# Block products over ten feature tiles in place of eight, with each column's weights in a chunk of its own

## The reference

```python
# first block
y = (o.astype(z.dtype) * jax.nn.silu(z)) @ w_out
x = x + rmsnorm(y, g_post[i])
# second block, for l in range(2)
y = jnp.concatenate([a_out, c_out, m_out], axis=-1) * jax.nn.silu(gate)
o = y @ w_o[l]
x = x + rmsnorm_2(o, post_norm_g[l])
```

## Time and profile before

| what | value |
|---|---|
| median of three runs | 2197.26 us (2196.68 to 2197.3) |
| the profiled execution, its own time | 2197.51 us |
| span of the profiled execution | 2195.7 us |
| TensorE busy | 2178.5 us (99%) |
| VectorE busy | 1524.7 us (69%) |
| ScalarE busy | 837.5 us (38%) |
| GpSimd busy | 211.3 us (10%) |
| mean granted TensorE clock | 0.999 of full speed |

### The profile page before, as it was taken

How to read it: one execution, slowest core, us unless ns; L and a number is a source line. 1 busy time by engine, 2 the same in 40 slices (tenths; PEclk the granted TensorE clock), 3 DMA queues, 4 the chain that set the end, 5 groups by cost and what they waited for, 6 DMA issues and landing times.

```text
span 2195.7 us, 27821 instructions
## 1 busy us (share of the span) xinstructions
PE 2178.5 (99%) x10428; PEld 1818.9 (83%) x10428; DVE 1524.7 (69%) x2224; ACT 837.5 (38%) x1307; POOL 211.3 (10%) x215
## 2 busy tenths in 40 slices
PE   8999999999999999999999999999999999999998
PEld 7888888888888888888888888888888888888887
DVE  6677788888988543567677778786434677677665
ACT  6433433453345421334333533444213443435221
POOL 0100000114420100000000053201000000000000
PEclk9999999999999999999999999999999999999999
DMA  7445545442257223225443422573222154435532
GB/s 278 172 154 155 159 157 160 146 149 96 89 213 273 78 96 100 75 75 160 134 139 119 142 107 82 194 268 113 96 96 75 65 158 132 144 117 155 176 119 108
DMA packets 91019, 303.25 MB, mean 138 GB/s; under 512 B 7536, under 2 KB 48752, under 8 KB 67888
## 3 DMA queue, kind: packets, MB, share of 16 engines
q1 hardware_dynamic: 84912, 275.00, 38.0%
q10 hardware_dynamic: 4896, 17.30, 2.1%
q0 software_dynamic: 1120, 9.70, 1.2%
HBM read 253.74 MB, written 48.23 MB: 138 GB/s over the span
## 4 chain that ended last, share of the span: by engine, by line
PE 98%; DMA 1%; DVE 1%; issue 0%; ACT 0%; SPq 0%; DVEq 0%; POOLq 0%; POOL 0%; ACTq 0%
PE acc L631 69%; PE sc L631 11%; PE ov L631 6%; PE sc L855 3%; PE sc L856 2%; PE ov L795 1%; PE sc L782 1%; PE sc L781 1%; PE sc L1038 1%; PE sc L1037 1%; DMA g<-xT_dram 0%; PE acc L816 0%; PE acc L817 0%; PE acc L647 0%; PE acc L820 0%
## 5 line engine op out<-in xcount | busy, mean ns | idle before, releaser
L631 PE MATMUL acc<-h_all,hi 128*128 128x512 f32 x4160 | 1286.9, 391 | 8.9 <-DVE h_all L1691 8.9
L631 PEld LDWEIGHTS acc<-h_all,hi 128*128 128x128 f32 x4160 | 775.6, 188 | 170.5 <-issue 12.0
L631 PE MATMUL acc<-h_all,lo 128*128 128x512 f32 x2080 | 809.9, 389 | 0.0
L1599 DVE TENSOR_TENSOR lo<-raw,hi 128x2048 fp32r<-128x2048 f32 (+3 forms) x158 | 345.1, 2184 | 171.3 <-ACT hi L1147 169.2
L631 PEld LDWEIGHTS acc<-h_all,lo 128*128 128x128 f32 x2080 | 390.8, 188 | 81.9
L1147 ACT ACTIVATE hi<-raw 128x2048 fp32r<-128x2048 f32 (+3 forms) x158 | 289.1, 1830 | 430.5 <-PE acc L631 263.8
L1229 ACT ACTIVATE prob<-prob,st 128x256 f32<-128x256 f32 x128 | 63.6, 498 | 109.4 <-DVE st L1752 109.4
L631 PE MATMUL sc<-hi,h_all 128*128 128x512 f32 (+1 forms) x320 | 90.7, 369 | 0.0
L1306 ACT ACTIVATE hi<-raw 128x512 fp32r<-128x512 f32 x50 | 30.4, 627 | 120.7 <-PE sc L856 107.5
L631 PEld LDWEIGHTS sc<-hi,h_all 128*128 128x128 f32 x320 | 58.1, 189 | 10.4 <-issue 0.5
L1542 ACT ACTIVATE prob<-sc,st 128x512 f32<-128x512 f32 x64 | 44.2, 690 | 43.6 <-DVE st L2299 43.6
(11 more groups left out here) (331 smaller groups left out, 3399.3 us busy)
## 6 DMA issues: line engine op xcount, KB each, us to landing
raw<-w_dram SPq DMA_DIRECT2D x170, 1024.0 KB, 4.9
turned<-pt SPq DMA_DIRECT2D x32, 512.0 KB, 3.2
pt<-turned SPq DMA_DIRECT2D x64, 256.0 KB, 5.1
turned<-pt SPq DMA_DIRECT2D x32, 448.0 KB, 3.0
pt<-turned SPq DMA_DIRECT2D x64, 224.0 KB, 4.0
xr<-residual ACTq DMA_DIRECT2D x16, 512.0 KB, 5.2
residual<-g ACTq DMA_DIRECT2D x16, 512.0 KB, 4.7
raw<-w_dram SPq DMA_DIRECT2D x8, 896.0 KB, 6.6
```

The costliest lines, as they stand in the source:

```text
L631: ins = pe.matmul(to, a, b, start=first and n == 0, stop=last and n == 2)
L1599: dve.tensor_tensor(lo[c.slot][:, 0:width], raw[c.slot][:, 0:width], hi[c.slot][:, 0:width].bitcast(F32), ALU.subtract).then_inc(lo_done, 1)
```

## The change

The block part takes ten feature tiles (8 to 15, and 6 and 7), the rest six (0 to 5). A block has five tiles in place of four (`NK` = 5, units of 640 columns in place of 512). Each chunk now holds one output column: its two blocks (`LEFT`, `RIGHT`: even and odd block tiles) and its rest (`REST`, 768 columns); before, a half of chunk d had 1024. Feature tiles 6 and 7 need activation sums of their own: `last_turned_sums` on GpSimd (four additions of 256 columns), `t5_hi` on ScalarE, `t5_lo` on VectorE, and TensorE's product 2 waits for them too. The two groups of `turned_sums` now stand behind one another, ahead of the first addition of squares. Since s1 is made of the second column's blocks, `weight_sums` waits for both loads, and it now stands behind the fold after product 6. A first column's rest is rounded before the units that come from sums. The core of the diff:

```diff
-    SU, TW, TILES = 512, 2048, S // 2
+    NK, TW, TILES = 5, 2048, S // 2
+    SU, BLOCK_TILES = NK * P, tuple(range(KT // 2, KT)) + (6, 7)
...
-        UNIT = tuple(slice(n * SU, (n + 1) * SU) for n in range(4))
-        HALF = (slice(0, CW // 2), slice(CW // 2, CW))
+        LEFT, RIGHT, REST = slice(0, SU), slice(SU, 2 * SU), slice(2 * SU, CW)
...
                 turned_sums(l, 0)
+                turned_sums(l, 1)
                 add_first_squares(sqacc, sq_no(l, POSTN))
-                turned_sums(l, 1)
+                last_turned_sums(l)
...
-                for m in range(4):
+                for m in range(NK):
...
-                for k in range(KT // 2):
+                for k in range(KT - 2 * NK):
...
-                pe.wait_ge(t_low, l * 4 + 4)
+                pe.wait_ge(t_low, l * 5 + 5)
...
-                unit_high(c, UNIT[0], w[:, A11], unit_hi)
-                act.wait_ge(chunk_done, c.n - 1)
+                unit_high(c, LEFT, raw[c.slot][:, LEFT], unit_hi)
+                second()
                 act.wait_ge(s_sum, no * 4 + 2)
-                unit_high(c, UNIT[1], s_two[:, 0:SU], unit_hi)
-                unit_high(c, UNIT[2], s_two[:, SU:2 * SU], unit_hi)
+                act.wait_ge(chunk_done, d.n - 2 if q > Q0 else d.n - 1)
+                unit_high(d, LEFT, s_two[:, 0:SU], unit_hi)
+                unit_high(c, RIGHT, s_two[:, SU:2 * SU], unit_hi)
...
+                dve.wait_ge(loaded[d.slot], (d.uses + 1) * 16)
+                if q > Q0:
+                    dve.wait_ge(unit_lo, (no - 1) * 5 + 3)
+                dve.tensor_tensor(s1, two[:, LEFT], two[:, RIGHT], ALU.add).then_inc(s_sum, 1)
                 dve.wait_ge(loaded[c.slot], (c.uses + 1) * 16)
-                dve.tensor_tensor(s1, w[:, A21], w[:, A22], ALU.add).then_inc(s_sum, 1)
...
                 fold(fix[0][:, 0:TILES], 1)
-                if more:
-                    weight_sums(l, q + 1)
                 dve.wait_ge(product_done, no * 6 + 6)
                 fold(fix[0][:, TILES:S], 3)
                 if more:
+                    weight_sums(l, q + 1)
                     first_unit_lows(l, q + 1, 0)
                 dve.wait_ge(chunk_done, c.n + 1)
                 fold(fix[1][:, 0:TILES], 2)
                 if more:
                     first_unit_lows(l, q + 1, 1)
-                    last_weight_sum(l, q + 1)
+                    first_rest_low(l, q + 1)
                     first_unit_lows(l, q + 1, 2)
```

194 lines of the change are left out of this document (107 added, 87 removed).

## The result

The changed kernel takes **2201.35 us** (median of 18 runs, 2200.52 to 2203.82), the kernel before 2197.28 us on the same chip (18 runs, 2196.2 to 2199.21): 4.1 us more, a ratio of 1.0018 (95% interval 1.0011 to 1.0026). The forecast was 2201.9 us. The difference is clear of the noise and lies just inside the 0.2% that the prediction counted as no change. The profiled execution of the changed kernel took 2201.74 us, at a granted clock of 0.999.

What follows compares the result with a forecast made beforehand. The prediction took TensorE's own work to bound the output products, with a loop of loads and VectorE setting the pace after the change. Its terms, -2.5 + 5.2 + 1.0 + 0.9 = +4.6 us, gave 2201.9 us, range 2196.3 to 2208.

Steps and rivals of the forecast that it cites:

- TensorE's own work: In the ten pairs of the output products: each falls by 0.25 us to 20.53, together -2.5 us.
- loop of load and sums: Between pairs: VectorE's 13.5 us plus 8.1 us of loads make 21.6 us, over TensorE's 20.53; +5.2 us.
- beginning: First pair of each output product: product 2 waits for its first unit, 0.1 us and 0.9 us late; +1.0 us.
- end: Behind product 7 of the last pair: the shorter rest makes tile 14's plain product 0.45 us late, twice; +0.9 us.
- What bounds the kernel: Inside both output products: every microsecond of TensorE's own work (99% busy) counts, the other engines are hidden behind it.
- the landing of the second load: In the loop: from the first load's issue to the second's landing, 8.1 us, with 7.1 and 9.2 as range.
- The count of the spare time: First pair: next load issued 8.4 us after product 1 starts, leaving 0.8 us to spare (0.6 in the second product).
- two small instructions of the angle (0.9): VectorE in the first product's first pair, behind the units: two small instructions counted at 0.9 us.
- the second load comes in time: Rival for the loop: loads take 7.1 us, loop 20.6 us, total 2196.9 to 2198.3 us, no change; chance 0.27.
- even if VectorE is free: Beginning of an output product: through ScalarE's split and the unit's tail, product 2 is 0.1 us late regardless of VectorE.
- What costs nothing: List counted at 0: ScalarE's wider units, the `lo` of the moved second rest, and its rounding moved to the pair's front.

Runs made afterwards that it cites:

- kernel 1: Changed kernel with the `lo` of the second column's rest moved behind the two units that the loads wait for: 2198.51 us, ratio 1.0006 to the kernel before.
- Kernels 1 and 2: The second of them: changed kernel with one more VectorE instruction of 512 columns, its result unread, in each pair transition: 2206.29 us, ratio 1.0040 to the kernel before.
- kernel 11: Changed kernel with the rest's `lo` later, chunk 14 split early, and GpSimd's tile 2 square addition held back in the second output product: 2196.80 us.
- kernels 3 and 5: Changed kernel with ScalarE splitting chunk 14 behind product 6, not 7: 2201.32 us; the same plus the second rest's `lo` behind the two units: 2197.62 us.

## Why the prediction was right, and where it wasn't

Undisturbed, the pair is 20.57 us. With that, the 2.72 us that the two output products lost can be laid out by the prediction's own terms (us):

| term | forecast | measured | from |
|---|---|---|---|
| TensorE's own work | -2.5 | -2.1 | ten pairs, 20.78 to 20.57 |
| loop of load and sums | +5.2 | +2.7 | steps above 20.57 behind the first pair, and the first step of the first product above kernel 1's (0.16): 0.9 and 1.8 |
| beginning | +1.0 | +1.1 | first step of kernel 1 above 20.57: 0.2 and 0.9 |
| end | +0.9 | +1.0 | tile 14 at 21.05 and 21.12 behind product 1 |
| elsewhere | 0 | +1.5 | the other three stretches |
| sum | +4.6 | +4.2 | |

- **What bounds the kernel.** Right: a microsecond of TensorE's in an output product counts, and VectorE, with 69% busy, became the limit for a part of a pair only. Kernels 1 and 2 show both directions.
- **TensorE's gain.** A tile of a block product is 0.353 us also with ten tiles. In an undisturbed pair of kernel 1 (from 551.84) products 1 to 3 take 5.29 us, the first rest 4.09 and products 4 to 7 take 7.05, as the tiles give; the 0.04 us more lie in the second rest, 4.14 us to the next product 1. Why is open.
- **The loop.** The mechanism was right, and VectorE's part of it to the tenth (13.5 us counted, 13.5 measured in six turns). The mis-sized term is the landing of the second load, "I take 8.1 us, the middle of 7.1 and 9.2". Measured from the first issue to the second landing are 7.1 to 7.3 in five of the ten pairs (issues 0.6 to 0.8 us apart), 7.5 and 8.0 in two more, and 8.1 to 8.6 in three. The count of the spare time was off as well, in the other direction: the first load of the second pair is issued 9.6 us behind product 1 and not 8.4, so the first step is late already. Rows of the changed kernel say why (below): the first of the "two small instructions of the angle (0.9)" takes 1.53 us, with a GpSimd addition of 512 columns beside it. In the kernel before it takes 0.41 (L1904 at 509.3), with none beside it. That is 1.1 us, once more the price of one addition. The two sizes partly cancel, and 5.2 became 2.7. The rival "the second load comes in time" came nearer in its size (7.1) than in its result, since 13.5 + 7.3 is still 0.2 above 20.57.

```profile
513.66 1.67 POOL L501 TENSOR_TENSOR sqacc<-sqacc,sq 128x512 f32<-128x512 f32 x1 [8.46 <-ACT sq L1180]
...
514.09 1.53 DVE L1938 CAST cs<-posi 128x512 f32<-128x512 int32 x1
```

- The Trainium skill ("DMA: Bandwidth & Descriptors", Anatomy of one DMA) has 2.0 us plus the bytes at 436 GB/s, a fit that the section gives for loads that GpSimd issues; SyncE issues these, which the prediction passed over. From it comes an estimate of 6.8 us for the second of two loads from the first one's issue. No pair here does with it; the nearest are 0.3 above, the farthest 1.8. By the skill's figure the loop would have been 20.3 us and cost nothing.
- **The beginning.** Right in size and in kind: additions of GpSimd beside VectorE's work make product 2 of the second output product late. The four of 256 columns that the change adds run from 1277.23 to 1282.5, and the `lo` of a unit beside them takes 1.36 us (1277.88) and not 0.81, as counted. The one of 512 columns that kernel 11 holds back isn't new: before, it ran beside a unit for which nothing waited (1277.77, 1.78 us), and now beside `t_parts`, where it counts. The rest of the term, product 2 at 1.91 us behind product 1 where five tiles are 1.77, is the chain by way of ScalarE that the prediction put at 0.1 us "even if VectorE is free". It is in the rows of the changed kernel's first output product, at the weight load of product 2:

```profile
512.76 0.19 PEld L874 LDWEIGHTS sc<-t_parts,hi 128*128 128x128 f32 x1 [0.32 <-DVE lo L1974]
```

- **The end.** Right: 0.5 us in each product, and gone when the chunk is split earlier (kernels 3 and 5). Another 0.12 us are lost within tile 14's product, three or four matmuls in; they stand under "elsewhere" in the table and go with the same edit.
- **"What costs nothing"** is the list that was incomplete. The prediction looked at the ten pairs alone; 1.5 of the 4.2 us lie elsewhere, all but the 0.12 twice in stages that the change doesn't touch. 0.18 up to the first output product is within what executions differ by there (509.96 to 511.96 in the fourteen kernels). The 0.8 behind the first product is in all ten-tile kernels and in none of eight tiles (0.6 to 1.1 over them). In the changed kernel 0.4 us of it appear at one matmul of the memory stage (at 661.69 in the kernel before). Part of it is a weight load that lands about 1 us later in its stage, seen in the trace; that a piece of program takes its place on a DMA engine was only argued. The 0.5 behind the second product is within what executions differ by: that stretch takes 799.37 to 800.17 us in the three eight-tile kernels and 799.42 to 800.68 in the ten-tile ones.

The time came out 0.6 us under the forecast because an overestimate of 2.5 us in the loop met 1.5 us that weren't foreseen. The mechanism in the output products was right and is shown; the nearness of the number is luck to a good part.

**Where the gain went.** Kernel 11 has lost nearly all waits of TensorE in the pairs: steps 20.78 and 20.57 throughout the second output product, which is 0.86 us shorter than before (103.07 and 103.93). Its time is that of the kernel before, 0.9997 (0.9988 to 1.0006). So the change can be brought back to even with three moved steps (the second rest's `lo`, the split of chunk 14, one addition of GpSimd), and what it would give with no waits at all, some 2 us in 2200, stays below what can be measured here.

## What to carry to other kernels

When a sum starts to need a second load, look for the loop: sum, `lo` that frees the slot, next load, sum. Add its two parts up and compare them with TensorE's time for a turn; an engine with 30% idle time can still set the pace there, and each microsecond of its work in the loop then counts for every turn. A kernel that is limited by such a loop gives a removed wait back later, so undo the loop first and test the other edits on top of that. And a change in one stage is checked by cutting the whole timeline at the same instructions before and after: a third of this difference lay outside the two stretches that the forecast was about. Compare it with how much the same stretch differs between runs of one code before looking for its cause.

## What the runs showed of the hardware that was not expected

- Two loads of 1 MiB that one queue issues 0.7 us apart: the first lands after 4.7 to 4.9 us in nearly all cases, the second 7.1 to 7.5 us after the first issue in most (8.0 and 8.6 in two). Issued 1.3 us apart, the second lands 8.1 and 8.3 us after the first issue.
- s1 waited for the same load at 528.51 and 528.55 us in two kernels with another order of work. When an engine waits for a load, where its instruction stands doesn't matter until the load is there, but what is then put behind it does.
- One GpSimd addition of 512 columns beside VectorE cost VectorE 1.1 us in two places: 3.99 us in place of 2.89 for two instructions of 1024 columns (kernel 11), and 1.53 in place of 0.41 for a cast of 512 columns with one input.
- A packet of 16 KB of the instruction queue (61 in each execution) falls within a weight load of 768 KB in each ten-tile kernel, and this load lands after 5.0 to 5.6 us; where it falls behind the load, the load lands after 4.1 or 4.2. Whether the one makes the other is open.
